# Router of three token chunks: three float32r products on split operands in place of one 32-bit product

## What is computed

```python
h = layer_norm(x, ln_in_g, ln_in_b)
mix = hybrid_mixer(h, w_in, pool_w, pool_scale, conv_w, conv_b, w_out)
h = layer_norm(ALPHA * h + mix, ln1_g, ln1_b)
# router, inside grouped_moe
probs = jax.nn.softmax((x @ w_router).astype(jnp.float32), axis=-1)   # 16 experts in 4 groups
# best group by the sum of its top two, then the top two experts of it
ffn = grouped_moe(h, w_router, router_bias, exp_w1, exp_w3, exp_w2)
out = layer_norm(ALPHA * h + ffn, ln2_g, ln2_b)
```

## Time and profile before

| | |
|---|---|
| median of three runs | 1367.25 us |
| the profiled execution's own time | 1365.61 us |
| its span, first to last instruction | 1363.6 us |
| TensorE matmuls (PE), busy | 1317.3 us, 97% |
| TensorE weight loads (PEld), busy | 1101.3 us, 81% |
| VectorE (DVE), busy | 958.1 us, 70% |
| ScalarE (ACT), busy | 512.3 us, 38% |
| GpSimd (POOL), busy | 520.1 us, 38% |
| mean granted TensorE clock, share of full speed | 0.992 |

### The profile page before, as it was taken

How to read it: one execution, slowest core, us unless ns; L and a number is a source line. 1 busy time by engine, 2 the same in 40 slices (tenths; PEclk the granted TensorE clock), 3 DMA queues, 4 the chain that set the end, 5 groups by cost and what they waited for, 6 DMA issues and landing times.

```text
span 1363.6 us, 20422 instructions
## 1 busy us (share of the span) xinstructions
PE 1317.3 (97%) x6386; PEld 1101.3 (81%) x6387; DVE 958.1 (70%) x1353; ACT 512.3 (38%) x570; POOL 520.1 (38%) x544
## 2 busy tenths in 40 slices
PE   4999999999999999999999999999999999999994
PEld 4988888888888888787788888888888888888883
DVE  7667667697759685788588875765675677776573
ACT  2433233322343233324345543442533445434340
POOL 1001110121101110021466665656566666666564
PEclk9999999999999999998999999999999999999997
DMA  9525444464455345624977774564554545666411
GB/s 265 161 78 164 147 123 170 155 193 118 154 183 158 108 139 174 212 95 147 350 264 263 262 253 162 172 237 147 181 195 184 189 176 210 239 232 230 138 54 63
DMA packets 156522, 243.58 MB, mean 179 GB/s; under 512 B 18944, under 2 KB 84992, under 8 KB 156480
## 3 DMA queue, kind: packets, MB, share of 16 engines
q1 hardware_dynamic: 118624, 154.15, 34.7%
q0 software_dynamic: 28928, 71.74, 14.9%
q10 hardware_dynamic: 8928, 17.13, 3.7%
HBM read 211.97 MB, written 64.62 MB: 203 GB/s over the span
## 4 chain that ended last, share of the span: by engine, by line
PE 93%; DVE 2%; issue 1%; DMA 1%; POOL 1%; POOLq 0%; ACT 0%; SPq 0%; DVEq 0%; ACTq 0%
PE acc L507 28%; PE acc L509 28%; PE acc L508 28%; PE tp L540 4%; PE logits L579 1%; PE aux L781 1%; DMA xg<-h_scratch,gat_now 1%; PE logits L727 1%; DMA b_in<-in_ln_in_b 0%; PE aux L509 0%; PE aux L508 0%; PE aux L507 0%; PE aux L619 0%; DVE hres L1099 0%; DVE xt_lo L1430 0%
## 5 line engine op out<-in xcount | busy, mean ns | idle before, releaser
L507 PE MATMUL acc<-ring_hi 128*128 128x512 f32 (+1 forms) x800 | 309.3, 387 | 4.4 <-DVE ring_lo L1126 4.4
L509 PE MATMUL acc<-ring_hi,ring_lo 128*128 128x512 f32 (+1 forms) x800 | 306.0, 382 | 0.0
L508 PE MATMUL acc<-ring_lo,ring_hi 128*128 128x512 f32 (+1 forms) x800 | 305.8, 382 | 0.0
L507 PE MATMUL acc<-ring_hi,xt_hi 128*128 128x512 f32 x640 | 253.4, 396 | 4.6 <-DVE xt_lo L1430 4.6
L509 PE MATMUL acc<-ring_hi,xt_lo 128*128 128x512 f32 x640 | 250.2, 391 | 0.0
L508 PE MATMUL acc<-ring_lo,xt_hi 128*128 128x512 f32 x640 | 250.1, 391 | 0.0
L1643 POOL TENSOR_TENSOR small<-small 128x1 f32<-128x1 f32 x32 | 46.9, 1467 | 364.5 <-DVE small L1093 364.5
L507 PEld LDWEIGHTS acc<-ring_hi 128*128 128x128 f32 x800 | 151.8, 190 | 32.3 <-DVE ring_lo L1126 4.8
L509 PEld LDWEIGHTS acc<-ring_hi,ring_lo 128*128 128x128 f32 x800 | 151.7, 190 | 29.1
L508 PEld LDWEIGHTS acc<-ring_lo,ring_hi 128*128 128x128 f32 x800 | 151.8, 190 | 27.6
L832 ACT CAST ring_hi<-stage_x 128x2048 fp32r<-128x2048 f32 x64 | 119.5, 1917 | 76.6 <-PE acc L509 76.1
(11 more groups left out here) (251 smaller groups left out, 1872.7 us busy)
## 6 DMA issues: line engine op xcount, KB each, us to landing
stage_x<-in_exp_w SPq DMA_DIRECT2D x64, 1024.0 KB, 6.6
stage<-in_w_in SPq DMA_DIRECT2D x64, 512.0 KB, 5.4
stage<-in_exp_w SPq DMA_DIRECT2D x32, 1024.0 KB, 6.5
stage<-in_w_out SPq DMA_DIRECT2D x32, 512.0 KB, 5.2
h_scratch<-hres POOLq DMA_DIRECT2D x16, 512.0 KB, 3.0
sum_scratch<-hres ACTq DMA_DIRECT2D x16, 512.0 KB, 2.9
hrow<-in_x POOLq DMA_DIRECT2D x12, 512.0 KB, 4.7
h_scratch<-hrow POOLq DMA_DIRECT2D x12, 512.0 KB, 3.0
```

The source lines that it names most:

```text
L507: nc.tensor.matmul(dst, w_hi, x_hi, start=start, stop=False)
L508: nc.tensor.matmul(dst, w_hi, x_lo, start=False, stop=False)
L509: return nc.tensor.matmul(dst, w_lo, x_hi, start=False, stop=stop)
```

## The change

Each transposed tile of the first three chunks' router is stored in a high part `h1t_hi` (ScalarE, in the place of the plain copy) and a low part `h1t_lo` (VectorE, `h1t_low`, two subtractions a tile). `w_router` gets a high and a low part once, in the first chunk. `route_tile` calls `three` for each of its eight steps. TensorE's waits for the copy (`s_h1tc`) become waits for the low part (`s_h1tlo`). `h1t_lo` has its place in two planes of `mix_v[1]` that are free in these units, so the last `pooled_split` of a chunk waits for the logits. The small vectors move to `small` to make room. The router of the fourth chunk stays as it was.

```diff
--- before.py
+++ after.py
@@ -141,6 +141,9 @@
         tri = sb("tri", [P, EPG, EPG])
         small = sb("small", [P, 64])
         small_at = nc.sbuf_base - 4 * 64
+        cw = small[:, 32:44].rearrange("p (w g) -> p w g", g=NG)
+        cb, ps = small[:, 44:48], small[:, 48:52]
+        zhist = small[:, 52:60].rearrange("p (g k) -> p g k", g=NG)
         stats = small[:, 0:12].rearrange("p (a b) -> p a b", a=2)
         mv, vareps, rstd, half = small[:, 12:14], small[:, 14:15], small[:, 15:16], small[:, 16:17]
         gate_0, lack = small[:, 17:18], small[:, 18:19]
@@ -188,14 +191,13 @@
         sum_a_at = m.at - 4 * (HIST + CHUNK)
         sum_b = m("sum_b", [P, HIST + CHUNK])
         sum_b_at = m.at - 4 * (HIST + CHUNK)
+        cacc = m("cacc", [P, CHUNK])
         zext = m("zext", [P, CONV_W - 1 + CHUNK])
-        cacc = m("cacc", [P, CHUNK])
         vhist = m("vhist", [P, NG, HIST])
-        zhist = m("zhist", [P, NG, CONV_W - 1])
         edge = m("edge", [P, NG, HIST])
-        cw = m("cw", [P, CONV_W, NG])
-        cb = m("cb", [P, NG])
-        ps = m("ps", [P, NG])
+
+        wr_hi = m("wr_hi", [P, KT, NE], F32R)
+        wr_lo = m("wr_lo", [P, KT, NE], F32R)
 
         pw_raw = h1t[:, 0:NG, :]
 
@@ -331,8 +333,13 @@
 
 
         ht_v = [a[:, RING1:RING1 + 2, :].rearrange("p u (k t) -> p (u k) t", t=CHUNK) for a in (ring_hi, ring_lo)]
+        h1t_hi = Place(h1t_at, h1t_at + 4 * D)("h1t_hi", [P, KT, P], F32R)
         mix_v = [a[:, RING1 + 2:RING, :].rearrange("p u (k t) -> p (u k) t", t=CHUNK) for a in (ring_hi, ring_lo)]
 
+
+        h1t_lo = [mix_v[1][:, k, :].rearrange("p (q t) -> p q t", t=P) for k in (NG - 1, 2 * NG - 1)]
+        s_wr = sem("router_split")
+        s_h1tlo = sem("h1_t_lo")
         s_gin = sem("ln_in_loaded")
         s_const = sem("const_loaded")
         s_cset = sem("const_set")
@@ -547,7 +554,7 @@
                 if not (isinstance(c, int) and c == 0 and t < 2):
                     pe.wait_ge(s_trlo, (c * TPC + t) * 2)
                 if t == 0 and c > 1:
-                    pe.wait_ge(s_h1tc, (c - 1) * TPC * 2)
+                    pe.wait_ge(s_h1tlo, (c - 1) * TPC * 2)
 
                 transpose_tile(hres[:, t, :] if isinstance(c, int) and c == 0 else hrow[:, t % 2, :], s_tr,
                                first_banks[t] if isinstance(c, int) and c == 0 else tp)
@@ -568,15 +575,17 @@
 
                 pe.wait_ge(s_h1, c * TPC + t + 1)
                 if t >= 1:
-                    pe.wait_ge(s_h1tc, (c * TPC + t) * 2)
+                    pe.wait_ge(s_h1tlo, (c * TPC + t) * 2)
                 transpose_tile(hres[:, t, :], s_h1t)
 
             def route_tile(c, t):
-                pe.wait_ge(s_h1tc, (c * TPC + t + 1) * 2)
+                pe.wait_ge(s_h1tlo, (c * TPC + t + 1) * 2)
+                pe.wait_ge(s_wr, 2)
                 tile = (c * TPC + t)
                 dst = logits[:, bass.ds(tile * NE, NE)]
                 for k in range(KT):
-                    mm = nc.tensor.matmul(dst, h1t[:, k, :], wr[:, k, :], start=(k == 0), stop=(k == KT - 1))
+                    mm = three(dst, h1t_hi[:, k, :], h1t_lo[k // 4][:, k % 4, :], wr_hi[:, k, :], wr_lo[:, k, :],
+                               k == 0, k == KT - 1)
                 mm.then_inc(s_log, 1)
 
             LAST = NCH - 1
@@ -875,7 +884,7 @@
                 for b in range(2):
 
                     act.wait_ge(s_h1t, (c * TPC + t) * 2 + b + 1)
-                    nc.scalar.copy(h1t[:, 4 * b:4 * b + 4, :], tp[b][:]).then_inc(s_h1tc, 1)
+                    nc.scalar.copy(h1t_hi[:, 4 * b:4 * b + 4, :], tp[b][:]).then_inc(s_h1tc, 1)
 
             def alpha_h1(c, t):
 
@@ -911,6 +920,7 @@
                     if first and j == 1:
                         act.wait_ge(s_const, 16 * N_CONST)
                         nc.scalar.copy(pw_hi[:], pw_raw).then_inc(s_pw, 1)
+                        nc.scalar.copy(wr_hi[:], wr[:]).then_inc(s_wr, 1)
                     if not first and 3 <= j < 7:
                         h1t_copy(c - 1, j - 3)
                     if not first and 4 <= j < 8:
@@ -1169,7 +1179,16 @@
                 ch.link(V.scalar_tensor_tensor(out=cacc[:], in0=zext[:, 0:CHUNK], scalar=cw[:, 0, g:g + 1],
                                                in1=cacc[:], op0=ALU.mult, op1=ALU.add))
 
+            def h1t_low(c, t):
+                for b in range(2):
+                    dve.wait_ge(s_h1tc, (c * TPC + t) * 2 + b + 1)
+                    V.tensor_tensor(h1t_lo[b], tp[b][:], h1t_hi[:, 4 * b:4 * b + 4, :].bitcast(F32), ALU.subtract)\
+                        .then_inc(s_h1tlo, 1)
+
             def pooled_split(c, g):
+                if c >= 1 and g == NG - 1:
+
+                    dve.wait_ge(s_log, c * TPC)
                 dve.wait_ge(s_pohi, c * NG + g + 1)
                 V.tensor_tensor(mix_v[1][:, g, :], sum_a[:, HIST:], mix_v[0][:, g, :].bitcast(F32),
                                 ALU.subtract).then_inc(s_polo, 1)
@@ -1331,6 +1350,8 @@
                     if j == 8 and not first:
                         route_shift(c - 1)
                     unit_ahead(c, j, last)
+                    if not first and 3 <= j < 7:
+                        h1t_low(c - 1, j - 3)
                     if j == 0 and c >= 2:
                         route_hots(c - 2)
                     if j == 1 and c >= 2:
@@ -1339,6 +1360,8 @@
                     if first and j == 1:
                         dve.wait_ge(s_pw, 1)
                         V.tensor_tensor(pw_lo[:], pw_raw, pw_hi[:].bitcast(F32), ALU.subtract).then_inc(s_pw, 1)
+                        dve.wait_ge(s_wr, 1)
+                        V.tensor_tensor(wr_lo[:], wr[:], wr_hi[:].bitcast(F32), ALU.subtract).then_inc(s_wr, 1)
                     if j < 8 and j % 2 == 0:
                         z_rows(c, g)
                         if g > 0:
```

## The result

The changed kernel takes **1393.44 us** (median of five runs, 1387.72 to 1394.39) against 1367.20 us (five runs, 1366.12 to 1369.74). The ratio is 1.0173, with a 95% interval from 1.0156 to 1.0190: 26 us slower, where 10 were forecast. The profiled execution took 1393.72 us with a span of 1391.7 us. Its span is 28.1 us longer than the one of before, and it is this difference that the profile has to explain.

What follows compares the result with a forecast made beforehand. The prediction took TensorE's issue time as the bound: 1365.61 us profiled + 10.2 for router products = 1375.8, with the median 1.64 above the profiled execution, so 1377.5 us; all else at nothing. Range 1374.5 to 1383.0 us.

Steps and rivals of the forecast that it cites:

- TensorE's issue time is the bound in the route stretches: In the router stretches, time is the sum of what TensorE issues; VectorE and ScalarE work is free if in time.
- Loads set a narrow product's price, float32r or not: In route tiles, each product costs 0.106 us; 24 take 2.55 us in place of 1.70, +10.2 us over twelve tiles.
- The 0.12 us of 256-column products: Rival on route tiles: width and load add up, so a product costs 0.12 us; 1381.5 us, chance 0.08.
- VectorE's cover: The low parts' 24 subtractions, 15.5 us of VectorE work, end before TensorE asks, with 1.4 us to spare; cost 0.
- The clock falls: Rival: longer narrow stretches at route tiles halve TensorE's clock, 1.5 us a fall, +18 over twelve tiles; 1395 us, chance 0.05.
- The fast rivals: Two cases of cheaper float32r products in route tiles, making the kernel faster: 1362.1 us and 1355.1 us, chance 0.03 each.
- The rule of four passes: Rival on route tiles: true 32-bit takes four passes, so three products save a quarter, -5.1 us; 1362.1 us, chance 0.03.
- The rival of the short load: Rival on route tiles: a float32r weight load is as short as float16's, up to -12.4 us; 1355.1 us, chance 0.03.
- The second half as long as it was: Sign of being right: the mixer ends 10.2 us later and the time behind it doesn't change.
- It comes out even: Rival: the extra TensorE time is given back where TensorE later waits for DMA or VectorE; 1367 us, chance 0.03.

Runs made afterwards that it cites:

- the plain-product run: The changed kernel with eight plain 32-bit products a route tile again, the low part computed but left out of the product: 1367.67 us, ratio 1.0003.
- the run with the transposes apart: The changed kernel with the next tile's transposes issued between the two sections of the next unit, not behind the router products: 1394.63 us, ratio 1.0177.
- The kernel with 48 wide products: The kernel before with 16 more 512-column products at the end of unit 7 in each of three chunks, into a free bank: 1381.08 us, ratio 1.0098.

## Why the prediction was wrong, step by step

- **That TensorE's issue time is the bound in the route stretches** held: it has no wait there after the change either.
- **Loads set a narrow product's price, float32r or not** held: 0.108 us measured, 0.106 forecast; twelve tiles 10.8 us, 10.2 forecast. The 0.12 us of 256-column products was indeed not paid, and at 128 columns the spacing was 0.110.
- **VectorE's cover** held: 15.5 us forecast and measured, no wait, and the plain-product run shows no cost (ratio 1.0003, 0.9985 to 1.0020).
- **The step that failed is the rival "The clock falls", held at 0.05 and left out of the range.** The row that I used against it was evidence for it. Between 610.72 and 621.41 the granted clock was full, and I took this as a sign that a narrow run is harmless, though the very next products ran at 1.2 GHz. The clock comes down at the end of such a run or behind it, so a full clock in the run itself is no sign that it is harmless. I also compared the stretches by length with their transposes, 3.4 us against 10.7; the run with the transposes apart shows that the router products suffice, and the run with 128 moving columns that length alone doesn't do it: it takes products that move little. A fall was priced at 1.5 us and cost 1.71; I had all twelve tiles at 18 us, and eight tiles came to 13.7. That this rival's 1395 us lies so near the measured 1393.44 is luck in part: it counted four falls too many and left out 0.6 us of the loads and the 5.1 us behind the mixer.
- **The fast rivals** fell. A plain 32-bit product is two matmuls here, each with the same spacing as a float32r one, so three split products with this stationary operand cost 3 x 0.108 = 0.324 us where one plain product costs 0.212. The rule of four passes (the Trainium skill, FP8 and Floating Point Precision, "TensorE Precision Notes") would have made the change a gain; what was measured goes the other way. The rival of the short load fell with the spacing of 0.108 us; its own figure was also 0.2 us off (1367.25 - 12.4 is 1354.9, not 1355.1).
- **"The second half as long as it was"** failed by 5.1 us in the first profile, 0.8 us in the second. The reason given for it, that TensorE's waits there hang on its own products, isn't what the earlier trace rows say: they name VectorE's `xt_lo` and `mask`. The kernel with 48 wide products was 9.7 us later at the mixer's end and 5.9 longer behind it, but whether the shift did that isn't shown.
- **The range** left out more than the 0.11 that was said: "It comes out even" at 1367 us lies outside it too, which makes 0.14.

## What to carry to other kernels

Count weight loads, not products: with 16 moving columns each of the three products costs a full load (0.108 us here), so put high and low parts side by side in the moving operand, or make the narrow operand the stationary one. Look at the granted clock of the products behind every run of narrow ones, because most of this cost shows there and not in the run; moving more columns behind the same loads cost 0.03 us a router tile and kept the clock up in the mixer. Compare clocks over several executions and not in one profile alone. And leave room in a range for a mechanism that one row of the profile already shows at work.

## What the runs showed of the hardware that was not expected

- Runs of 24 products with 16 moving columns (2.6 us) brought the clock to half behind eight of twelve tiles in two profiles of the changed kernel and in the one with the transposes apart, and behind five in the kernel before with 24 plain passes. Each fall cost 1.71 us. Runs of 16 (1.7 us) did so behind none in the mixer. Behind it, four tiles of 16 such matmuls with little but transposes between them, the last two back to back (3.49 us), were followed by a fall at 621 us, which was gone when they moved 128 columns.
- The same 24 loads with 128 columns moving took 2.63 instead of 2.60 us and brought no fall in the mixer.
- Float32r products that load 32 columns and move 128 start 0.06 us apart; those that load 128 and move 128 start 0.110 apart.
